# Two-block transformer layer stack: scores and turns set between chunks of the next head's units, and a new order of latent sums

## What is computed

```python
h = rms_norm_2(x, mix_norm_g[layer])
proj = h @ w_in[layer]
da_q, da_k, da_v, sb_q, sb_k, sb_v, c_q, c_kv, k_r = jnp.split(proj, pts, axis=-1)
y_a = diff_attention(...)      # 4 heads; q and k in two halves of 64, v of 128
y_b = stick_breaking(...)      # 4 heads of 64
y_c = latent_attention(...)    # 4 heads, 64 + 32 rotated
x = x + jnp.concatenate([y_a, y_b, y_c], axis=-1) @ w_out[layer]

# diff_attention
q = rms_norm_2(q.reshape(b, s, DA_HEADS, 2, DA_DIM), q_g)
k = rms_norm_2(k.reshape(b, s, DA_HEADS, 2, DA_DIM), k_g)
p = jax.nn.softmax(logits, axis=-1)          # logits = q k / 8 + bias, masked by chunks of 64
a = p[:, :, 0] - lam * p[:, :, 1]
o = rms_norm_2(a @ v, subln_g) * (1.0 - lam_init)

# latent_attention
q = rms_norm_2(q, q_g)
k = rms_norm_2(k, k_g)
q = concatenate([q[..., :MLA_NOPE], rope(q[..., MLA_NOPE:], pos)])
```

## Time and profile before

| | us |
|---|---|
| median of 3 runs | 3553.13 |
| lowest and highest | 3548.35, 3557.21 |
| the profiled execution, its own time | 3550.04 |
| its span, first to last instruction | 3548.2 |
| PE busy | 3166.5 (89%) |
| DVE busy | 1626.1 (46%) |
| ACT busy | 1455.8 (41%) |
| POOL busy | 759.2 (21%) |

### The profile page before, as it was taken

One profiled execution on the slowest core, in us unless ns is written; L12 is line 12 of the kernel. 1 busy time (PEld: TensorE's weight loads), 2 busy tenths in 40 slices (PEclk: granted clock), 3 DMA queues, 4 the chain that ended last, 5 costly groups with the idle time before them and its releaser, 6 DMA issues.

```text
span 3548.2 us, 43654 instructions
## 1 busy us (share of the span) xinstructions
PE 3166.5 (89%) x13571; PEld 2479.1 (70%) x13571; DVE 1626.1 (46%) x2425; ACT 1455.8 (41%) x2128; POOL 759.2 (21%) x320
## 2 busy tenths in 40 slices
PE   7999999799997757999968978699998897879998
PEld 5788887588885545888746756488876664658887
DVE  4544544666565437565556344421125535351113
ACT  3333333433344545343344555432334455442323
POOL 1233232000002310000021212144432111214442
PEclk8999999899998878999978989799998898979999
DMA  8322222233331212333221211133332111213332
GB/s 201 96 86 78 66 86 60 76 96 96 94 90 42 74 45 83 93 93 95 65 78 36 55 48 42 30 95 93 92 88 85 48 53 33 60 29 93 94 94 77
DMA packets 486165, 269.41 MB, mean 76 GB/s; under 512 B 9418, under 2 KB 477458, under 8 KB 485620
## 3 DMA queue, kind: packets, MB, share of 16 engines
q1 hardware_dynamic: 479236, 255.85, 25.6%
q10 hardware_dynamic: 6768, 11.62, 1.0%
HBM read 264.12 MB, written 12.21 MB: 78 GB/s over the span
## 4 chain that ended last, share of the span: by engine, by line
issue 54%; PE 29%; POOL 11%; DVE 3%; ACT 2%; DMA 0%; SPq 0%; POOLq 0%; ACTq 0%; DVEq 0%
POOL s_w_lo L625 11%; PE acc L664 8%; PE acc L665 8%; PE acc L670 7%; PE acc L667 1%; PE wide L691 1%; PE misc L938 1%; PE misc L665 0%; PE misc L664 0%; PE misc L670 0%; PE wide L664 0%; DMA s_raw<-attn_w_qkv 0%; SPq L520 0%; DVE s_sc L2022 0%; POOLq L102 0%
## 5 line engine op out<-in xcount | busy, mean ns | idle before, releaser
L625 POOL TENSOR_TENSOR s_w_lo<-s_raw,s_w_hi 128x1024 fp32r<-128x1024 f32 x316 | 759.0, 2402 | 2760.3 <-ACT s_w_hi L1236 2755.2
L664 PE MATMUL acc<-s_h_hi,s_w_hi 128*128 128x512 f32 (+1 forms) x2128 | 873.5, 410 | 119.5 <-POOL s_w_lo L625 44.4
L665 PE MATMUL acc<-s_h_lo,s_w_hi 128*128 128x512 f32 (+1 forms) x2128 | 847.0, 398 | 0.0
L670 PE MATMUL acc<-s_h_hi,s_w_lo 128*128 128x512 f32 (+1 forms) x1862 | 741.3, 398 | 0.0
L664 PEld LDWEIGHTS acc<-s_h_hi,s_w_hi 128*128 128x128 f32 x2128 | 409.1, 192 | 238.2 <-issue 73.0
L1236 ACT ACTIVATE s_w_hi<-s_raw 128x1024 fp32r<-128x1024 f32 x388 | 411.7, 1061 | 387.1 <-DVE s_x L2527 210.9
L665 PEld LDWEIGHTS acc<-s_h_lo,s_w_hi 128*128 128x128 f32 x2128 | 410.5, 193 | 94.9 <-issue 7.1
L670 PEld LDWEIGHTS acc<-s_h_hi,s_w_lo 128*128 128x128 f32 x1862 | 358.6, 193 | 83.9
L664 PE MATMUL acc<-s_hid_hi,s_w_hi 128*128 128x512 f32 x752 | 297.4, 395 | 0.0
L665 PE MATMUL acc<-s_hid_lo,s_w_hi 128*128 128x512 f32 x752 | 297.3, 395 | 0.0
L670 PE MATMUL acc<-s_hid_hi,s_w_lo 128*128 128x512 f32 x658 | 260.0, 395 | 0.0
(11 more groups left out here) (395 smaller groups left out, 4875.3 us busy)
## 6 DMA issues: line engine op xcount, KB each, us to landing
s_raw<-w_ff SPq DMA_DIRECT2D x128, 512.0 KB, 4.0
s_raw<-ffn_w_up SPq DMA_DIRECT2D x96, 512.0 KB, 3.9
s_raw<-attn_w_qkv SPq DMA_DIRECT2D x72, 512.0 KB, 3.6
s_raw<-ffn_w_down SPq DMA_DIRECT2D x48, 512.0 KB, 3.9
s_raw<-w_in SPq DMA_DIRECT2D x44, 512.0 KB, 4.0
s_raw<-lru_w_in SPq DMA_DIRECT2D x16, 512.0 KB, 3.9
s_raw<-w_out SPq DMA_DIRECT2D x16, 512.0 KB, 4.0
s_raw<-attn_w_o SPq DMA_DIRECT2D x8, 512.0 KB, 4.1
```

Source lines behind the costliest of these rows:

```text
L625: pool.tensor_tensor(w_lo_of[w][:], raw_b[s][:], w_hi_of[w][:].bitcast(F32), ALU.subtract).then_inc(sems["unit_ready"], 1)
L664: mm(out, ahi, bhi, start=start, stop=False, **kw)
L665: mm(out, ahi, blo, start=False, stop=False, **kw)
L670: mm(out, alo, bhi, start=False, stop=stop, **kw)
```

## The change

On all three engines the differential heads are written in a new order. Before the loop stand the three units of head 0, with the keys' sum inside the unit of values. In the loop, head h's eight scores stand ahead of the eight chunks of the next head's queries' unit; then come the next keys' unit, the sum of the queries' squares, and the next values' unit, with head h's four turns ahead of chunks 0, 2, 4, 6 and the keys' sum ahead of chunk 3; then value products, turn_v and the output's sum. In the last head the "next" units are the first three of the stick-breaking heads, and the output's sum moves into the first stick-breaking head. ACT squares keys before it takes the queries' root. In the latent heads the order of sums becomes queries (in `misc`), keys (in an acc bank of their own), rotation; and keys are scaled and cut ahead of queries.

Core of the diff ("..." stands for what is left out; parts of the PE, ACT and DVE programs in this order):

```diff
-                for h in range(HEADS_2):
-                    unit_of(h_hi, h_lo, before=...)
-                    if h == 0:
-                        stats()
-                    unit_of(h_hi, h_lo)
-                    head_sum(HALVES)
-                    if h:
-                        turn_a()
-                    unit_of(h_hi, h_lo)
-                    head_sum(HALVES)
-                    if h:
-                        weigh_values()
-                    turn_v()
-                    pe.wait_ge(sems["hn_lo"], count("hn_lo", 2))
-                    for q in range(TT):
-                        for m in range(2):
-                            ...
-                    if h:
-                        head_sum(ONES)
-                turn_a()
-                weigh_values()
-                head_sum(ONES)
+                next_unit(lambda k: pe.wait_ge(sems["h_lo"], count("h_lo")))
+                stats()
+                next_unit()
+                head_sum(HALVES)
+                next_unit(da_keys_sum)
+                turn_v()
+                for h in range(HEADS_2):
+                    pe.wait_ge(sems["hn_lo"], count("hn_lo", 2))
+                    next_unit(da_scores)
+                    next_unit()
+                    if h < HEADS_2 - 1:
+                        head_sum(HALVES)
+                        next_unit(da_turn_and_sum)
+                        weigh_values()
+                        turn_v()
+                        head_sum(ONES)
+                    else:
+                        next_unit(da_turn)
+                        weigh_values()
...
                 def mla_sums():
+                    head_sum(ONES, MLA_W, squared="mla_sq")
+                    pe.wait_ge(sems["mla_sq"], count("mla_sq"))
+                    if past := count("acc_freed", lag=count.banks):
+                        pe.wait_ge(sems["acc_freed"], past)
+                    mm(bank[count.bank()][0:MLA_W, :], square[0:MLA_W, ONES, 0:MLA_W], sq[0:MLA_W, 1, :], start=True,
+                       stop=True).then_inc(sems["acc_full"], 1)
...
-                    head_sum(ONES, MLA_W, squared="mla_sq")
-                    head_sum(ONES, MLA_W, first=1, squared="mla_sq")
```

```diff
+                def da_keys():
+                    head_rstd(SUB)
+                    head_hi(kh[:], tn[:, 1, :])
+                def da_queries():
                     output()
                     head_square(tn[:, 0, :])
                     output()
+                    head_square(tn[:, 1, :], part=1)
                     head_rstd(SUB)
                     head_hi(qh[:], tn[:, 0, :], SUB ** -0.5)
...
+                    if h < HEADS_2 - 1:
+                        da_queries()
+                        turned_a()
+                        da_keys()
+                        output()
+                        count("po_freed")
+                        square_output()
+                        turned_v()
                         norm_output(P)
+                    else:
+                        sb_hi(0)
+                        sb_hi(1)
+                        turned_a()
+                        output()
+                        count("po_freed")
+                        square_output()
```

```diff
+                for h in range(HEADS_2):
+                    da_scores(h)
+                    if h < HEADS_2 - 1:
+                        o = output()
+                        scaled(tn[:, 0, :], o[:])
+                        da_weights()
+                        o = output()
+                        scaled(tn[:, 1, :], o[:])
+                        da_queries()
+                        turned_a()
+                        da_keys()
+                        values()
+                        take_output()
+                        turned_v()
+                        da_output(h)
+                    else:
+                        sb_lo(0)
+                        da_weights()
+                        sb_lo(1)
+                        turned_a()
+                        values()
+                        take_output()
```

More of the change, by code:

```diff
@@ L267, in build_program @@
             "hn_sq hn_rstd hn_norm hn_hi hn_lo po_full po_freed a_mid rot_full "
-            "l_sum mla_norm kr_in rope_done mla_sq l_abs l_done z_full a_exp sq32 ".split())
+            "l_sum mla_norm mla_ln kr_in rope_done mla_sq l_abs l_done z_full a_exp sq32 ".split())
         sems = {n: ctx.enter_context(nc.semaphore(n)) for n in names}
@@ L963, in weigh_values @@
                               "po_full" if j == TT - 1 else None)
[L966 to L986 removed]
+                next_unit = lambda before=None: unit_of(h_hi, h_lo, before=before)
@@ new lines, in da_scores, with da_turn @@
+                def da_scores(k):
+                    q, m = divmod(k, 2)
+                    w = (q + 1) * P
+                    o, r = next_wide(), slice(q * P, w)
+                    three(o[:, 0:w], qh[half(m), r], ql[half(m), r], kh[half(m), 0:w], kl[half(m), 0:w],
+                          True, True, "wide_full")
+                def da_turn(k):
+                    q = k // 2
+                    if k % 2 == 0:
+                        pe.wait_ge(sems["p_ready"], count("p_ready"))
+                        turn4(next_wide(), [sd[:, 0, TRI[q] + j * P:TRI[q] + (j + 1) * P] for j in range(q + 1)], "wide_full")
@@ L1038, in memory_kv, with last_sum_and_unit @@
                     unit_of(m_hi, m_lo, N_MEM, (lambda k: pe.wait_ge(sems["m_lo"], count("m_lo"))) if n == 0 else None)
-                next_unit = lambda: unit_of(h_hi, h_lo)
-                for _ in range(3):
+                def last_sum_and_unit():
+                    head_sum(ONES)
                     next_unit()
-                sb_heads(next_unit, lambda scores: unit_of(h_hi, h_lo, before=scores), next_unit, next_unit)
+                sb_heads(last_sum_and_unit, next_unit, next_unit, next_unit)
                 next_unit()
@@ L1720, in mla_hi @@
                     head_rstd(MLA_W, MLA_W)
-                    head_rstd(MLA_W, MLA_W, dst=sd[0:MLA_W, 1, S:2 * S])
+                    rs_k = sd[0:MLA_W, 1, S:2 * S]
+                    act.wait_ge(sems["acc_full"], count("acc_full"))
+                    fn(rs_k, bank[count.bank()][0:MLA_W, :], ACT.Ln, bias=eps[0:MLA_W, 0:1], scale=1.0 / MLA_W).then_inc(sems["mla_ln"], 1)
+                    count("acc_freed")
+                    count.outs += 1
+                    act.wait_ge(sems["mla_ln"], count("mla_ln"))
+                    fn(rs_k, rs_k, ACT.Exp, scale=-0.5).then_inc(sems["hn_rstd"], 1)
+                    act.wait_ge(sems["hn_rstd"], count("hn_rstd"))
+                    freed()
+                    fn(mla_k[h % 2][0], kr[0:MLA_W, :], ACT.Copy).then_inc(sems["hn_hi"], 1)
+                    act.wait_ge(sems["hn_hi"], count("hn_hi"))
                     count("acc_full")
@@ L2311, in sb_heads @@
                     take_output(slice(SUB, P))
-                def sb_lo(j):
-                    lo, hi, scale = ((ql, qh, SUB ** -0.5), (kl, kh, 1.0))[j]
-                    o = output()
-                    scaled(tn[:, j, :], o[:])
-                    head_lo(lo[:], tn[:, j, :], hi[:], scale)
-                def values():
-                    o = output()
-                    scaled(vt2[:], o[:])
                 def fill_cq(n):
```

114 lines of the change are left out of this document (53 added, 61 removed).

## The result

The changed kernel took 3622.89, 3623.68 and 3627.41 us; the kernel before, measured beside it, 3552.49 (median of 4). A fourth execution of the changed kernel took 4232.94 us, at a mean granted clock of 0.702 where the others have 0.91, and is left out of every comparison. The ratio is 1.0203, with a 95% interval of 1.0183 to 1.0223: slower, by about 2%, some 71 us. The forecast was 3572 in a range of 3532 to 3594, some 19 us above the kernel before. The direction was right; the loss was well over three times as large.

The account below looks back on a forecast made before the run. Differential heads were taken as bound by a chain over DVE and ACT, with PE's work beside it. Per layer 15.4 + 0.9 - 5.6 = +10.7, over two layers +21.4 on 3550.04: 3572 us, range 3532 to 3594.

Parts of the forecast that it names:

- the stage: Differential heads up to softplus, per layer: softplus moves from 1964.79 to 1980.2, +15.4 us.
- the three periods: Gaps between first scores of heads 1 to 4: 41.2 us each, the first 40.0, putting head 4 at 1944.1.
- T to S: From a head's first score starting (T) to its last score landing (S): 12.5 us, with 3.9 in crossings.
- S to softplus: Last head, from its last score landing to softplus: 22.8 us, with weights slowed by POOL.
- S to W: From the last score landing to the end of the weights (W): 11.0 us, two POOL stalls at 2.35 each.
- W to the next T: From the end of the weights through keys, values and output's sum to the next head's first score: 15.15 us.
- clean period: One differential head, first score to next first score, before clock loss: 12.5 + 11.0 + 15.15 = 38.65 us against 33.15.
- latent sums: Latent heads' new order of sums: scores start sooner, -5.6 us per layer, bounds -2 to -8.
- The clock: New idle spells in differential heads lower TensorE to 1.2 GHz: 2.5 us lost a head; bounds nothing or 3.4 each.
- rival 3: Each idle spell is followed by 10 us at half clock: 12 us more a layer, 3596 us; chance 0.05.
- Rival 2: Crossings and POOL as walked, but the clock stays up: +2.1 us a layer, 3554 us; chance 0.24.
- The spell before the keys' sum: In the values' unit PE waits for ACT's queries' logarithm to free the misc bank: idle 3.9 us.

Follow-up runs that it names:

- experiment 5: Changed kernel plus unread matmuls filling TensorE's idle spells: 3570.4 us; with the spells ahead of the first head's scores filled too, 3553.7 us.
- experiment 1: Kernel before with only the new order of latent sums, differential heads as they were: 3539.8 us against 3550.3, ratio 0.9969.
- experiment 9: Kernel before with the new latent sums and only the last differential head overlapped with three stick-breaking units: 3521.4 us, ratio 0.9899.
- experiment 4: Changed kernel with the output's sum of heads 1 to 3 moved behind the next head's unit with scores: 3572.6 us, ratio 1.0054.

## Why the prediction was right or wrong

The loss by parts, layer 0, in the terms of the forecast: the stage was to grow by 15.4 us and grew by 40.0. Of the 24.6 between them, 18.6 lie in the three periods, 7.0 in the last head's T to S, 0.7 ahead of head 1, and -1.6 from S to softplus.

**T to S, without the clock: right.** Forecast 12.5 with the crossings; at full clock (experiment 5) 11.6 was measured. A score of 512 columns and its chunk take 1.79 us between them, the two crossings 0.41 of it (six plain steps of 0.23 taken off), not 0.49. By the Trainium skill, TensorEngine Tiling (Array Packing), Key Properties, each of them drains TensorE, and the trace agrees in that a crossing costs 0.2 us beyond a plain step. The streaming of the eight scores was put at 3.8 to 3.9; at the 0.36 for 256 columns of the earlier trace rows it is 3.6.

**S to W: right.** Forecast 11.0, measured 10.6 to 11.0 in heads 1 to 3 and 12.5 in the last (forecast 12.6), with both POOL stalls.

**W to the next T: right at full clock.** Forecast 15.15, measured 15.36 in experiment 5; in the changed kernel 15.9 to 16.3, since sums at 1.2 GHz stand on that path. The clean period was forecast at 38.65 and is 37.6.

**The latent sums: right in sum, partly by luck.** Forecast -5.6 a layer, measured -5.3 to -5.5 (experiment 1). Counted from the keys' rotation, the first scores of the four heads come 5.0, 4.8, 6.4 and 6.2 earlier in the changed kernel, so the three later heads give about what was walked (0, 1.7 and 0.4), the first gives 5.0 and not 3.5, and some 1 us is lost again behind them.

**The last head: right in kind.** From S to softplus 22.8 was forecast and 21.2 came out. The overlap of three units, which I had put at 16.8 us of PE's time, makes the stage 11.6 us shorter a layer by itself (experiment 9), 9.2 by the medians of the program.

**The clock: here it failed.** The step is "Near the shorter row I take 1.3 for the first, 1.2 for the second: 2.5". Measured are 8.0 to 8.7 us in the unit with scores and 0.5 to 0.9 in the sums behind; in the program it is 70 us over eight heads, about 8.7 a head. The rows at low clock that I had the earlier trace rows were of a block of scores with plain work behind it; the one row of a mixture was at full clock. No row showed a mixture at low clock, so it was an unknown with its own upper bound, all of the 12.5 us at half clock. I closed the bounds at 6.8 us of low clock a spell instead, and rival 3, with 4 us more a head, was the same mistake in a milder form (its 3596 even lies outside the range, which ends at 3594). The trace of the kernel before had warned of more than both, in its own head 4:

```profile
1922.32:1942.80 20.48, 12.53 (x37) 8.18 (x36) 14.07 (x32) 9.20 (x24) 0.00 (x0) 0.50 0.02 5
```

Rival 2, clock up and all else as walked, was 3554, and the run that held the clock up gave 3553.7. That its mechanism fits is more than luck: the stage was to grow by 6.8 us a layer and grew by 6.5 and 7.3. That the total fits to 0.3 us is luck, since 3554 was counted from 3550.04 and the kernel beside that run took 3552.1, and since terms cancel: a period was 37.6 and not 38.65, while head 1 began 2.7 us later than walked (the extra matmuls stand ahead of it) and S to softplus took 22.5 where the rivals have 21.5.

**The spell before the keys' sum**, forecast at 3.9, was 0.97 to 2.08, because the slow unit delayed PE itself; with a fast unit ahead it was 3.20 (experiment 4). The two errors belong together: the low clock hid a wait that I had priced.

## What to carry to other kernels

Setting small 64-row matmuls between the chunks of a unit made that unit depend on TensorE's clock: where the clock fell at its start, it stayed low to its end. Pairs of opposite halves (3553.6) and a block (3546.7) avoided most of that here, and so did filling the idle spells ahead (3553.7). So look at the spells that stand ahead of such a unit. When a pattern is new to the trace, bound it at both clocks for its whole length, not by the low stretches of another pattern. Take an order apart before judging it: here one end of it (the overlap of the last head) and the latent sums were worth 1%, and the new order of the heads before that cost 3% (3521.4 against 3623.7).

## What the runs showed that I had not expected

- PE busy in every microsecond of a stretch of 23.85 us, at 1.2 GHz all the way. With the same spells ahead and 128-row scores, only 3.4 us (1 - 0.84 of 10.5, doubled) were low in head 1. The Trainium skill, TensorE: Matmul & The Clock Gate, Part 1: The HAM clock gate, has activity release the clock; here a stream in which PE was never idle did not release it for 23.85 us.
- The same mixture has two paces, 11.6 and about 20 us, according to whether the clock falls at its start; in experiment 4 both stand in one layer.
- Two scores in opposite halves of the array run at once (0.91 us for six matmuls of 512 columns, 0.88 for three). The old block of scores used this as well (the x2 of the earlier trace rows); the single scores of the change gave it up.
- Up to 30 extra matmuls a head, read by nobody, made the kernel 70 us faster.
